# Halves of projection tiles set between the turns of the attentions, keys rotated ahead of the queries' high parts, and the high parts of the first output inside the last dilated pass

## The reference, cut to what matters

```python
def hybrid_mixer(h, w_in, w_a, w_b, w_out, ...):          # first block, 2 layers
    z = h @ w_in                                          # q, k, v of 4 global heads; 3 dilation groups; gates
    qa, ka = apply_rope(...), apply_rope(...)             # 4 differential heads, 2 score maps each
    oa = differential_attention(qa, ka, va, lam_full, subln_g, lambda_init)   # "global output"
    for g, (window, dilation) in enumerate(DIL_GROUPS):   # (128,1), (512,4), (2048,16), 8 heads
        og, lg = dilated_window_attention(qg, kg, vg, dilation, ...)
    ob = weighted sum of the three groups                 # "local output"
    merged = gates[:, :, 0] * (oa @ w_a) + gates[:, :, 1] * (ob @ w_b)
    return merged @ w_out

def second_block(...):                                    # 2 layers
    y_a, y_b, y_c, y_d = pool, chunk band, top-k sparse, latent attention
    # sparse: score = sum_h iw * relu(iq . ik);  _, sel = top_k(score, 128);  softmax over the selected keys
```

## Time and profile before

| what | value |
|---|---|
| runs of the kernel before | 3375.14, 3363.87, 3376.1 us (median 3375.14) |
| the profiled execution's own time | 3365.66 us |
| its span | 3363.8 us (first to last instruction) |
| PE busy | 3233.6 us, 96% of the span |
| DVE, ACT, POOL busy | 1643.3 (49%), 1351.7 (40%), 1375.7 us (41%) |
| granted PE clock, mean | 0.992 of full speed |

### The profile page before, as it was taken

One profiled execution on the slowest core, in us unless ns is written; L12 is line 12 of the kernel. 1 busy time (PEld: TensorE's weight loads), 2 busy tenths in 40 slices (PEclk: granted clock), 3 DMA queues, 4 the chain that ended last, 5 costly groups with the idle time before them and its releaser, 6 DMA issues. The chain is left out here.

```text
span 3363.8 us, 46345 instructions
## 1 busy us (share of the span) xinstructions
PE 3233.6 (96%) x16177; PEld 2576.3 (77%) x16177; DVE 1643.3 (49%) x2609; ACT 1351.7 (40%) x2110; POOL 1375.7 (41%) x694
## 2 busy tenths in 40 slices
PE   7999999999998999999999999999999989999998
PEld 5677777788886677777788887767888867778887
DVE  5843335665635743335755633773333238533332
ACT  5755554322225755555322224454222234532222
POOL 2233333444443233333444444534444435444444
PEclk8999999999999999999999999999999999999999
DMA  3122221255532122222245533212222232023232
GB/s 130 56 79 80 83 78 63 81 180 194 212 106 72 56 79 80 82 78 68 83 175 195 210 107 103 76 32 72 97 96 99 97 112 76 32 76 100 94 104 102
DMA packets 94332, 335.82 MB, mean 100 GB/s; under 512 B 11236, under 2 KB 12132, under 8 KB 93968
## 3 DMA queue, kind: packets, MB, share of 16 engines
q1 hardware_dynamic: 92640, 328.12, 28.6%
q10 hardware_dynamic: 1584, 6.29, 0.5%
HBM read 332.22 MB, written 8.44 MB: 101 GB/s over the span
## 5 line engine op out<-in xcount | busy, mean ns | idle before, releaser
L434 POOL TENSOR_TENSOR wLo<-wring,wHi 128x1024 fp32r<-128x1024 f32 x482 | 1172.0, 2431 | 1770.2 <-ACT wHi L414 1770.0
L458 PE MATMUL psG<-hHi,wHi 128*128 128x512 f32 x2992 | 1181.7, 395 | 10.0 <-ACT whole L1817 4.0
L458 PE MATMUL psG<-hLo,wHi 128*128 128x512 f32 x2992 | 1169.8, 391 | 11.1 <-POOL hLo L483 10.2
L458 PE MATMUL psG<-hHi,wLo 128*128 128x512 f32 x2992 | 1165.7, 390 | 0.0
L414 ACT ACTIVATE wHi<-wring 128x1024 fp32r<-128x1024 f32 x482 | 511.0, 1060 | 976.9 <-PE psG L458 956.4
L458 PEld LDWEIGHTS psG<-hHi,wHi 128*128 128x128 f32 x2992 | 562.1, 188 | 149.8 <-issue 25.8
L458 PEld LDWEIGHTS psG<-hLo,wHi 128*128 128x128 f32 x2992 | 561.9, 188 | 142.7 <-POOL hLo L483 24.9
L458 PEld LDWEIGHTS psG<-hHi,wLo 128*128 128x128 f32 x2992 | 562.4, 188 | 114.1 <-issue 0.5
L458 PE MATMUL psG<-hidLo,wHi 128*128 128x512 f32 x704 | 273.9, 389 | 0.0
L458 PE MATMUL psG<-hidHi,wHi 128*128 128x512 f32 x704 | 273.9, 389 | 0.0
L458 PE MATMUL psG<-hidHi,wLo 128*128 128x512 f32 x704 | 273.9, 389 | 0.0
(11 more groups left out here) (323 smaller groups left out, 3476.4 us busy)
## 6 DMA issues: line engine op xcount, KB each, us to landing
wring<-in_w SPq DMA_DIRECT2D x494, 512.0 KB, 3.3
modw<-in_wmod SPq DMA_DIRECT2D x96, 512.0 KB, 5.3
e_copies<-e_rows ACTq DMA_DIRECT2D x8, 512.0 KB
T_tab<-e_copies SPq DMA_DIRECT2D x4, 1024.0 KB, 5.5
mask<-in_mask SPq DMA_DIRECT2D x2, 1536.0 KB, 6.2
xin_sb<-in_x SPq DMA_DIRECT2D x4, 512.0 KB, 5.1
e_copies<-e_rows ACTq DMA_DIRECT2D x8, 256.0 KB
out<-o_sb SPq DMA_DIRECT2D x4, 512.0 KB, 3.8
```

What stands on the lines that cost most here:

```text
L434: pool.tensor_tensor(wLo[:, c % CUTS, :, :], wring[:, c % RING, :, :], wHi[:, c % CUTS, :, :], ALU.subtract).then_inc(w_cut[c % CUTS], 1)
L458: mm = pe.matmul(psG[:, G.slot(u), :], w[:, c % CUTS, k, :], r(j), start=start and j == 0 and n == 0, stop=stop and j == len(kts) - 1 and ...
```

## The change

**Global heads.** On PE the 24 matmuls of the next head's keys are divided: 12 before `turn(3)` and 12 behind it. On ACT `cut_q` moves behind `next_rope(1)`; on DVE `rest_q` moves behind `next_rope(1)` as well.

**Dilated pass.** On PE tile 11 is divided: 18 matmuls (6 of the 8 k) before `scores(1)`, 6 between `turn(0)` and `turn(1)`. Tile 12 is divided: 6 matmuls (2 k) before `turn(6)`, 18 where all 24 were. On ACT `gate(11)` with its weight cut moves from before `out_T(0)` to behind `out_T(1)`. The last of the four passes is written out on ACT, and in it the four copies to oaHi stand before `gate(12)`.

**Top-k.** Of the rounds in step 7 two go away (3 to 1); one goes to the first point of step 8 (2 to 3), one to step 11 (0 to 1).

```diff
-TAKE_AT = {0: 5, 1: 4, 2: 5, 3: 4, 4: 4, 5: 1, 6: 1, 7: 3, 9: 4, 10: 2}
-TAKEN_LATENT = (2, 4)
+TAKE_AT = {0: 5, 1: 4, 2: 5, 3: 4, 4: 4, 5: 1, 6: 1, 7: 1, 9: 4, 10: 2, 11: 1}
+TAKEN_LATENT = (3, 4)
...
                        turn(2)
                        if not last:
-                            project(d_K, 5)
+                            project_first(d_K, 5)
                         turn(3)
+                        if not last:
+                            project_second(d_K, 5)
...
                        scores(0)
-                        tile(11, 10)
+                        tile_first(11, 10, 6)
                         for p in range(1, DL + 1):
                             if p < DL:
                                 scores(p)
+                            else:
+                                tile_first(12, 11, 2)
                             turn(2 * p - 2)
+                            if p == 1:
+                                tile_second(11, 10, 6)
                             if p >= 2:
                                 values(p - 2)
                             turn(2 * p - 1)
-                        tile(12, 11)
+                        tile_second(12, 11, 2)
                         values(DL - 1)
...
                        out_T(1)
                         out_T(2)
-                        if not last:
-                            cut_q(i * 2 + 3)
                         out_T(3)
                         if not last:
                             next_rope(1, d_K)
+                            cut_q(i * 2 + 3)
...
                        expo(0)
                         expo(1)
-                        gate(11, 1)
-                        follow(act, CH1_DL + 10, g_DL + 11, i, 12, GK_DL)
                         for p in range(1, DL + 1):
                             out_T(2 * p - 2)
                             if p < DL:
                                 expo(2 * p)
                                 expo(2 * p + 1)
                             out_T(2 * p - 1)
+                            if p == 1:
+                                gate(11, 1)
+                                follow(act, CH1_DL + 10, g_DL + 11, i, 12, GK_DL)
+                        if last:
+                            high_act(act, 0, tiles(oaT), tiles(oaHi), DA_HEADS, o_full, o_high)
                         gate(12, 2)
...
-                    high_act(act, 0, tiles(oaT), tiles(oaHi), DA_HEADS, o_full, o_high)
+                    with act.Fori(0, DL_PAIRS - 1) as i:
+                        local(i, False)
+                    local(DL_PAIRS - 1, True)
...
                            next_rope(0, d_Q)
+                            next_rope(1, d_K)
                             rest_q(i + 2)
-                            next_rope(1, d_K)
                             rest_k(i + 2)
```

More of the change, by code:

```diff
@@ L798, in attend, with project_first, project_second @@
                     def attend(i, last):
+                        half = KT // 2
                         def project(d, c):
                             gemm(pe, g_DA + d, CH1_DA + c, h, all_k, i, GK_DA, 4)
+                        def project_first(d, c):
+                            gemm(pe, g_DA + d, CH1_DA + c, h, range(half), i, GK_DA, 4, stop=False, used=False)
+                        def project_second(d, c):
+                            gemm(pe, g_DA + d, CH1_DA + c, (tiles(hHi, half), tiles(hLo, half)), range(half, KT), i, GK_DA, 4, start=False)
                         def scores(n):
@@ L854, in attend @@
                         mm.then_inc(G.filled(o), 1)
-                        half = KT // 2
                         if not last:
-                            gemm(pe, g_DA + d_V, CH1_DA + 6, h, range(half), i, GK_DA, 4, stop=False, used=False)
+                            project_first(d_V, 6)
                         pe.wait_ge(osq_full, i + 1)
@@ L865, in attend @@
                         if not last:
-                            gemm(pe, g_DA + d_V, CH1_DA + 6, (tiles(hHi, half), tiles(hLo, half)), range(half, KT), i, GK_DA, 4, start=False)
+                            project_second(d_V, 6)
                     with pe.Fori(0, DA_HEADS - 1) as i:
@@ L875, in tile, with tile_first, tile_second @@
                             gemm(pe, g_DL + j, CH1_DL + c, h, all_k, i, GK_DL, 12)
+                        def tile_first(j, c, k):
+                            gemm(pe, g_DL + j, CH1_DL + c, h, range(k), i, GK_DL, 12, stop=False, used=False)
+                        def tile_second(j, c, k):
+                            gemm(pe, g_DL + j, CH1_DL + c, (tiles(hHi, k), tiles(hLo, k)), range(k, KT), i, GK_DL, 12, start=False)
                         def turn_v(n, ring, ps, u, K):
@@ L1097, in _, with local @@
                     act.wait_ge(rows_out, 16)
-                    with act.Fori(0, DL_PAIRS) as i:
+                    def local(i, last):
                         for o, r, n in ((e_copies[l + 1], e_rows[l + 1], HEADS),
```

## The result

| | before | after |
|---|---|---|
| median of four runs | 3374.79 us (3363.87 to 3376.1) | **3337.63 us** (3334.54 to 3342.29) |
| the profiled execution, its span | 3365.66, 3363.8 us | 3335.76, 3334.0 us |

The ratio is 0.9898, 95% interval 0.9874 to 0.9922: 1.0% faster, by 37 us between the medians and 29.9 between the profiled executions. The difference between these two lies in before's level: in 25 further runs of before its median was 3365.97, 28.3 above the changed kernel's, so that some 9 of the 37 us are chance of the four runs in the table. The time goes with the granted clock of a run (3363.5 to 3367.4 at 0.991 to 0.993, 3371.2 to 3379.1 at 0.986 to 0.987). The two profiled executions both stood at 0.992, so the 29.9 us are compared place by place.

A forecast was written before the change was run, and what follows sets the result against it. It took PE, busy 96% of the span, as the bound, with only its waits able to move. Terms of 5.4, 12.8, 5.0 and 2.9 us gave 3339.6 us; set between two run levels, the forecast was 3344, range 3327 to 3359.

The forecast's parts named there:

- The sum of waits: Whole kernel: 5.4 + 12.8 + 5.0 + 2.9 = 26.1 us off the profiled execution's 3365.66, giving 3339.6 us.
- Dilated passes: Eight dilated passes: PE's waits at the turns go, 1.6 us a pass, 12.8 us in all.
- all three waits: PE's waits in a dilated pass: turn(1) 0.56 us, turn(6) 0.89, turn(2) 0.16; 1.61 a pass, all to go.
- each bracket: Dilated pass: each wait as the trace brackets it, taken about 0.08 us short of what the matmuls' pitch loses.
- The cover: Dilated pass: ACT's slots for turn(4) free at about 265.5, PE wants the first at 265.9; margin 0.3 to 0.4 us.
- First rival: Inside a dilated pass ACT and DVE become the bound; 1.6 us a pass goes to 0, 3352 us; chance 0.14.
- Heads: Six looped global heads: next scores start 0.9 us earlier through the keys' chain to kLo, 5.4 us in all.
- Behind the last pass: After each layer's last dilated pass: obLo ready 2.0 us earlier, 1.0 more in layer 0 by clock; 5.0 us.
- Rounds: Top-k rounds, two layers: 2.2 us won at step 8's turn, 0.75 lost at the scores behind step 11; 2.9 us.
- The level: Runs' median, 3375.14 us, stood 9.5 above the profiled execution; a new median may stand at either, so forecast between, 3344.
- Slower by the clock: Rival: PE's clock drops behind new short waits; in each of 14 heads and passes, 21 us slower, 3387; chance 0.04.

## Why the prediction was right, step by step

The direction, the order of the parts and the range held; the time lay 6 us under the forecast. The sum of waits was 26.1, measured 29.9 between the profiled executions.

- **Dilated passes, 12.8 forecast, 16.4 measured.** The mechanism held: all three waits went. Two things were mis-sized. I took 1.6 of a gross 1.85 and subtracted for the changes between tile work and turns; in the trace the six matmuls between `turn(0)` and `turn(1)` take 1.40 us, six of a tile 1.36. And I took each bracket to be 0.08 short of the wait. At `turn(1)` of the earlier trace rows it is 0.16 short: the turn starts 0.83 behind the matmul before it, and their pitch is 0.11. Three such waits make the 1.61 of the brackets 2.05. The cover held.
- **First rival** (ScalarE or VectorE the bound, 0.14). Its block shows in one row, 0.34 us on one scaling, and falls where 0.3 to 0.4 was left. The kernel with the gate's cut ahead shows what the order is worth: with the tiles divided and ScalarE's order kept, a pass takes 0.7 us more than before, and 2.0 more where the clock fell.
- **Heads, 5.4 forecast, 4.1 measured.** L853 at 117.8 and the wait of 0.32 at `turn(3)` came as worked out, and the keys' halves start 1.05 earlier in the head. The term fails where `cut_q` and `rest_q` together were given 0.1: `rest_q` pushes kLo back by 0.3 (kLo starts 1.63 behind the start of kHi, 1.31 before). The reasoning "the scores wait for kLo, so the chain to kLo is the bound" was wrong as a reason: taking that wait away alone gave nothing. Its size was near, 0.9 against 0.7 a head, and that was luck: kLo begins the queue on VectorE that is the bound, so a kLo that comes earlier moves the bound too. And the divided tile, to which the text gave the gain, gives none of it: the order on ScalarE does.
- **Behind the last pass, 5.0 forecast, 5.4 measured**, 3.2 with the clock in layer 0 and 2.2 in layer 1. obLo became the next to be late, as stated.
- **Rounds, 2.9 forecast, 3.4 measured.** Won 2.4 a layer (2.2 forecast), lost 0.7 (0.75 forecast).
- **The level.** I added 4.4 us to stand between two levels. The changed kernel's four runs had 0.990 to 0.993 and none stood at the upper one (0.986 to 0.987). Without that addition the sum says 3339.6, 2 us from the median; part of that nearness is luck too, since the terms together were 3.8 us short of the profiled difference and the four runs' median lies 1.9 above the profiled execution.
- **Slower by the clock (0.04).** It did not come at the places of the change, where no new wait is longer than 1.05 us. Behind waits of 2.31 and 1.71 us that I made elsewhere it came, in six passes of eight and in two layers of two.

## What to carry to other kernels

A long wait at one place in a loop need not be its bound: ask what its releaser does next and who waits for that, and test it by taking the wait away. When an edit has a half on each of two engines, try the halves apart: one may do it all, or one alone may be a loss. Of a round or a copy that is to fill idle time, find the idle time in the order of the code, not only on the clock, since a step too early it becomes a wait of TensorE and the clock can fall behind it. When two traces differ, follow them through to the end: a sum over the places of the change can meet the total while others cancel.

## What the runs showed of the hardware

- TensorE's granted clock behind a new wait. Behind one of 2.30 or 2.31 us in each dilated pass it fell in six passes of eight (0.84 and 0.74 in the two windows of 4 us shown), which cost 1.3 us beside the wait; in two it stayed at 1.00. Behind one of 1.71 us it fell both times (0.50 and 0.62 over ten microseconds), which cost 4.8 us. Behind the new waits of 0.3 to 1.05 us in the changed kernel's trace no fall is seen.
- Six 128x512 matmuls set between 128x128 turns cost TensorE 1.40 us, six inside a tile 1.36.
- A reciprocal of 128x256 takes VectorE 1.75 us, a subtraction of 128x512 from SBUF 0.7; GpSimd takes 1.25 to 1.3 for that subtraction.
